# A decoder layer step on one core: a projection that multiplies tiles as they arrive, and an expert stage whose down product takes 4-byte operands

## The reference

```
h  = rms_norm(x, g_mix)                       # rows, then times g_mix by column
p  = h @ w_in                                 # 1024 x 3072: qd kd vd | qs ks vs, 512 columns each
o  = concat(diff_attention(qd, kd, vd), stick_breaking_attention(qs, ks, vs))
x1 = x + o @ w_out
h2 = rms_norm(x1, g_ffn)
gates: top 1 of 4 groups, then top 2 of its 4 experts, softmax weights
y  = x1 + sum over the 2 experts of gate * ((silu(h2 @ w_gate[e]) * (h2 @ w_up[e])) @ w_down[e])
out = rms_norm(y, g_final)                    # and k and v rows of both kinds are outputs
```

## Time and profile before

| what | us |
|---|---|
| three timed executions | 1706.43, 1712.57, 1714.13 (median 1712.57) |
| the profiled execution, its own time | 1703.53 |
| its span, first to last instruction | 1701.7 |
| PE busy, mean granted clock | 1345.3, 0.901 |
| DVE, ACT, POOL busy | 817.5, 721.3, 267.8 |
| first product of project to its last result | 38.95 to 371.27 |
| attention of both kinds, mix_out, route | 378 to 1258 |
| experts, from the first gate_up to the last store's issue | 1280.68 to 1631.35 |
| combine, to the end | 1636 to 1701.7 |
| DMA | 319.76 MB, 188 GB/s over the span |

### The profile page before, as it was taken

How to read it: one execution, slowest core, us unless ns; L and a number is a source line. 1 busy time by engine, 2 the same in 40 slices (tenths; PEclk the granted TensorE clock), 3 DMA queues, 4 the chain that set the end, 5 groups by cost and what they waited for, 6 DMA issues and landing times. The chain is left out here.

```text
span 1701.7 us, 28599 instructions
## 1 busy us (share of the span) xinstructions
PE 1345.3 (79%) x8942; PEld 1004.4 (59%) x8942; DVE 817.5 (48%) x1142; ACT 721.3 (42%) x1115; POOL 267.8 (16%) x200
## 2 busy tenths in 40 slices
PE   6999999977878887858887878599428888899920
PEld 4777787755545555435555554488326667677720
DVE  7022112104645445527574758444346665567735
ACT  6022212204545364535454545223106676677711
POOL 1000000000000000000000000000004545566544
PEclk6999999998999899979999999799758999999975
DMA  5333123217867776367777778354136797643257
GB/s 190 96 118 124 68 69 112 79 57 254 254 216 260 219 247 218 118 210 250 225 215 247 230 246 271 91 173 149 74 140 244 294 354 301 234 176 108 91 193 300
DMA packets 165910, 319.76 MB, mean 188 GB/s; under 512 B 21607, under 2 KB 59018, under 8 KB 161674
## 3 DMA queue, kind: packets, MB, share of 16 engines
q1 hardware_dynamic: 152922, 275.06, 48.5%
q0 software_dynamic: 7200, 26.22, 4.3%
q10 hardware_dynamic: 5648, 16.78, 2.5%
HBM read 312.82 MB, written 56.03 MB: 217 GB/s over the span
## 5 line engine op out<-in xcount | busy, mean ns | idle before, releaser
L2011 PE MATMUL gate_up_ps<-w_gate_up_split,slot_rows_T 128*128 128x512 f32 x768 | 194.5, 411 | 31.8 <-DVE slot_rows_T L2063 31.7
L2055 DVE TENSOR_TENSOR w_gate_up_split<-w_gate_up,w_gate_up_split 128x2048 fp32r<-128x2048 f32 x64 | 143.8, 2289 | 131.7 <-ACT w_gate_up_split L2109 131.7
L1979 POOL TENSOR_TENSOR w_down_split<-w_down,w_down_split 128x2048 fp32r<-128x2048 f32 x32 | 170.5, 5328 | 162.1 <-ACT w_down_split L2117 162.1
L933 PE MATMUL turns_and_scores_ps<-ident,pages 128*128 128x128 f32 (+1 forms) x1088 | 151.6, 284 | 55.8 <-DMA pages<-in_cache_s 27.2
L2011 PEld LDWEIGHTS gate_up_ps<-w_gate_up_split,slot_rows_T 128*128 128x128 f32 x768 | 149.3, 198 | 70.2 <-DVE slot_rows_T L2063 38.6
L933 PEld LDWEIGHTS turns_and_scores_ps<-ident,pages 128*128 128x128 f32 (+1 forms) x1088 | 124.0, 148 | 99.1 <-issue 98.8
L255 PE MATMUL proj_ps<-w_in_hi,h_T_hi 128*128 128x512 f32 x432 | 173.6, 402 | 9.4 <-DVE w_in_lo L305 9.4
L255 PE MATMUL proj_ps<-w_in_lo,h_T_hi 128*128 128x512 f32 x432 | 170.8, 395 | 0.0
L255 PE MATMUL proj_ps<-w_in_hi,h_T_lo 128*128 128x512 f32 x432 | 170.6, 395 | 0.0
L2109 ACT ACTIVATE w_gate_up_split<-w_gate_up 128x2048 fp32r x64 | 119.0, 1907 | 120.3 <-DMA w_gate_up<-in_w_up 92.8
L350 ACT ACTIVATE proj_rows<-proj_ps,sum_squares 128x512 f32<-128x512 f32 x54 | 37.0, 688 | 276.2 <-PE proj_ps L255 259.1
(11 more groups left out here) (227 smaller groups left out, 2138.4 us busy)
## 6 DMA issues: line engine op xcount, KB each, us to landing
pages<-in_cache_d SPq DMA_DIRECT2D x256, 256.0 KB, 3.1
pages<-in_cache_s SPq DMA_DIRECT2D x256, 256.0 KB, 3.1
w_gate_up<-in_w_gate SPq DMA_DIRECT2D x32, 1024.0 KB
w_gate_up<-in_w_up SPq DMA_DIRECT2D x32, 1024.0 KB
w_down<-in_w_down SPq DMA_DIRECT2D x32, 1024.0 KB
scratch_moe_out<-expert_out ACTq DMA_DIRECT2D x32, 512.0 KB
w_in_now<-in_w_in SPq DMA_DIRECT2D x48, 256.0 KB, 4.6
x_tiles<-in_x SPq DMA_DIRECT2D x9, 512.0 KB, 10.5
```

Of the source, the lines that this page charges most:

```text
L933: last = pe.transpose(kT_ps[:, KIND_BLOCKS * e + b, 0:n], rows[0:n, e, b, :], t.ident[0:n, 0:n])
L1979: pool.tensor_tensor(dn_split[:, u, 1, :, :], w_dn[:, bass.ds(at, 1), :, :].rearrange("p a k n -> p (a k) n"), dn_split[:, u, 0, :, :].bit ...
L2011: last = pe.matmul(gu_ps[:, u, :], xT[:, u, a, k, :], gu_split[:, u, b, k, :], start=(k == 0 and m == 0), stop=(k == KC - 1 and m == 2))
L2055: dve.tensor_tensor(gu_split[:, u, 1, at, :].rearrange("p k (c n) -> p k c n", c=2), raw[:, at, :, :], gu_split[:, u, 0, at, :].bitcast(F3 ...
```

## The change

In project:

- The order of groups is k, q, v for each kind. Nine x tiles go through three places. PE turns tiles 0 and 1, then multiplies tile 0 with the first group; in each later step of the first group it turns the tile two ahead.
- g_mix goes into w_in and no longer into h: ACT scales by g when it makes the high part, DVE when it makes the low part. x is split straight from PSUM by ACT and DVE.
- w_in_hi and w_in_lo have two copies, and the next group's pieces are split one per step, during the first eight steps of a group.
- q is made as columns: a slice of 128 columns of w_in is the stationary operand, the x columns of all tiles are the moving one, in chunks of 512, 512 and 128; 12 steps for a group of q, no transposes. A column's factor (root of its row times 1/8) is needed along the free axis: ACT makes nine diagonal blocks, PE multiplies ones by them (1152 columns, 4-byte operands), ACT keeps the result, DVE multiplies by it.
- The bias tables' products and copies stand in steps 3 to 7 after the first group, their spreading on SyncE behind the first q group. The loop is written out.

In experts: the down product takes the raw w_down and the activations as 4-byte operands, four products of 512 in place of twelve; there is no split of w_down and none of the activations. Raw weights have four places, with one place number; the load of down waits for the down product of tile t - 4. PE loads the place number itself. keep_act comes before keep_y on ACT. In route the place is the turn number and 3 (six instructions fewer).

```diff
+GROUPS = [(kind, role) for kind in range(2) for role in ROLE_NAMES]
+X_PLACES = 3
+PJ_BANKS = 3
...
+        w_hi = sb("w_in_hi", [P, 2, KC, BANK], F32R)
+        w_lo = sb("w_in_lo", [P, 2, KC, BANK], F32R)
...
+                load_x(0)
+                for k in range(KC):
+                    load_w(0, k)
+                    if k in (2, 5):
+                        load_x(k // 2)
...
+                def product(step):
+                    g, a, c = step
+                    n = number[step]
+                    if g == 0:
+                        pe.wait_ge(lo_done, 2 * a + 2)
...
+                        if step == of_group[g][0]:
+                            pe.wait_ge(w_lo_done, g * KC + k + 1)
+                        if GROUPS[g][1] == "q":
+                            c0, c1 = CHUNKS[c]
+                            at = slice(a * P, a * P + P)
+                            for m, (w, h) in enumerate(((w_hi, hT_hi), (w_hi, hT_lo), (w_lo, hT_hi))):
+                                last = pe.matmul(pj_ps[:, n % PJ_BANKS, 0:c1 - c0], w[:, g % 2, k, at], h[:, k, c0:c1],
+                                                 start=(k == 0 and m == 0), stop=(k == KC - 1 and m == 2))
+                        else:
+                            at = slice(a * P, a * P + P)
+                            for m, (h, w) in enumerate(((hT_hi, w_hi), (hT_lo, w_hi), (hT_hi, w_lo))):
+                                last = pe.matmul(pj_ps[:, n % PJ_BANKS, :], h[:, k, at], w[:, g % 2, k, :],
+                                                 start=(k == 0 and m == 0), stop=(k == KC - 1 and m == 2))
...
+                turn_x(0)
+                turn_x(1)
+                unturned = None
+                for step in steps:
+                    g, n, _ = step
+                    product(step)
+                    if g == 0 and n + 2 < TILES:
+                        turn_x(n + 2)
+                    if unturned:
+                        turn_k(unturned)
+                    unturned = step if step in turned else None
+                    if number[step] >= last_of(0):
+                        after = number[step] - last_of(0)
+                        if after < len(CHUNKS) and after < 2:
+                            rstd_across(after)
+                        elif after == 2:
+                            rstd_across(2)
+                        elif after < 3 + H_DIFF + 1:
+                            tables.bias(pe, after - 3, row_kept)
...
+                def low_w(g, k):
+                    dve.wait_ge(w_hi_done, g * KC + k + 1)
+                    dve.scalar_tensor_tensor(w_lo[:, g % 2, k, :], w_raw[:, k, :], g_T[:, k:k + 1],
+                                             w_hi[:, g % 2, k, :].bitcast(F32), ALU.mult, ALU.subtract)\
+                       .then_inc(w_lo_done, 1)
+
...
+                    dve.tensor_tensor(qkT[:, m % 3, 0:c1 - c0], pj_ps[:, n % PJ_BANKS, 0:c1 - c0], rstd_row[:, c0:c1],
+                                      ALU.mult).then_inc(cols_kept, 1)
...
+                act.wait_ge(g_loaded, 16)
+                high_x(0)
+                for k in range(4):
+                    high_w(0, k)
+                high_x(1)
+                for k in range(4, KC):
+                    high_w(0, k)
+                high_x(2)
...
+                    if g == 0 and n + 2 < TILES:
+                        high_x(2 * n + 4)
+                        high_x(2 * n + 5)
+                        square(n + 2)
+                    if g == 1 and at < len(CHUNKS):
+                        keep_across(at)
+                    if step in in_rows:
+                        keep_rows(step)
+                    if g == 0:
+                        diagonal(n)
+                    if at < KC and g + 1 < len(GROUPS):
+                        high_w(g + 1, at)
+                    if g == 1 and at == len(CHUNKS) + 1:
+                        tables.exps_of_sums(act)
...
+W_PLACES = 4
...
-                    dn_lo.reached(sp, tile - DN_PLACES)
+                    y_done.reached(sp, tile - W_PLACES, 1)
...
-                    u = tile % 2
+                    u, at = tile % 2, place(pe, tile)
                     aT_kept.reached(pe, tile)
-                    dn_lo.reached(pe, tile)
+                    pe.wait_ge(dn_loaded[tile % W_PLACES], 16 * (tile // W_PLACES) + 16)
                     for c in range(2):
                         y_kept[c].reached(pe, tile - 1)
+                        own_wait(pe, t)
                         for k in range(FK):
-                            for m, (a, b) in enumerate(PRODUCTS):
-                                last = pe.matmul(y_ps[:, c, :], aT[:, u, a, k, :],
-                                                 dn_split[:, u, b, k, c * BANK:(c + 1) * BANK],
-                                                 start=(k == 0 and m == 0), stop=(k == FK - 1 and m == 2))
+                            last = pe.matmul(y_ps[:, c, :], aT[:, u, k, :],
+                                             w_dn[:, bass.ds(at, 1), k, c * BANK:(c + 1) * BANK]
+                                             .rearrange("p a n -> p (a n)"), start=(k == 0), stop=(k == FK - 1))
                         last.then_inc(y_done.sem, 1)
...
-                    split_dn(tile)
                     swish(tile)
                     if tile + 1 < MOE_TILES:
                         split_rows(tile + 1)
+                    keep_act(tile)
                     if tile:
                         keep_y(tile - 1)
-                    keep_act(tile)
                     if tile:
```

More of the change, by code:

```diff
@@ L38 @@
 BANK = 512
-PROJ_G = 3 * MIX_W // BANK
 BLOCKS = MIX_W // P
@@ L110, in sem @@
             return sems[-1]
[L112 to L117, removed]
-        g_T = sb("g_mix_T", [P, KC])
[L119 to L123, removed]
+        steps = project_steps()
@@ new lines, in project @@
+        number = {step: n for n, step in enumerate(steps)}
+        in_rows = {step: n for n, step in enumerate(s for s in steps if GROUPS[s[0]][1] != "q")}
+        in_cols = {step: n for n, step in enumerate(s for s in steps if GROUPS[s[0]][1] == "q")}
+        of_group = [[s for s in steps if s[0] == g] for g in range(len(GROUPS))]
+        turned = {step: n for n, step in enumerate(s for s in steps if GROUPS[s[0]][1] == "k")}
+        staged = {step: n for n, step in enumerate(s for s in steps if GROUPS[s[0]][1] != "v")}
@@ L147, in project, with last_of @@
         w_view = t.w_in.rearrange("(k p) n -> k p n", p=P)
[L148 to L156, removed]
+        tables = Tables(nc, ctx, sems, t, [xT_ps[:, n, :] for n in range(2)])
+        def last_of(g):
+            return number[of_group[g][-1]] + 1
         with nc.Block() as block:
@@ L234, in _, with turn_k @@
                         last.then_inc(xT_done, 1)
[L235 to L241 removed]
+                def turn_k(step):
+                    r, n = in_rows[step], turned[step]
+                    pe.wait_ge(rows_kept, r + 1)
+                    if n >= 3:
+                        pe.wait_ge(tr_kept, n - 2)
@@ L298, in _ @@
[L298 to L313 removed]
+                    at, cols = slice(4 * half, 4 * half + 4), slice(n * P, n * P + P)
@@ new lines, in _ @@
+                low_x(0)
+                for k in range(4):
+                    low_w(0, k)
+                low_x(1)
+                for k in range(4, KC):
+                    low_w(0, k)
+                low_x(2)
+                low_x(3)
+                unturned = None
+                for step in steps:
+                    g, n, _ = step
+                    at = number[step] - number[of_group[g][0]]
+                    if g == 0 and n + 2 < TILES:
+                        low_x(2 * n + 4)
+                        low_x(2 * n + 5)
+                    if unturned:
+                        keep_turned(unturned)
+                    unturned = step if step in turned else None
+                    if step in in_cols:
+                        keep_columns(step)
+                    if at < KC and g + 1 < len(GROUPS):
+                        low_w(g + 1, at)
+                    if step == of_group[0][-1]:
+                        tables.widen(dve)
+                    after = number[step] - last_of(0) - 3
+                    if 0 <= after < H_DIFF + 1:
+                        tables.keep(dve, after)
+                    if g == 2 and at == 1:
+                        tables.rest(dve)
```

424 lines of the change are left out of this document (202 added, 222 removed).

## The result

| | before | changed |
|---|---|---|
| median of four executions, us | 1713.09 (1706.43 to 1714.13) | 1655.43 (1652.47 to 1659.02) |
| profiled execution, span | 1701.7 | 1650.6 |
| PE, DVE, ACT, POOL busy | 1345, 817, 721, 268 | 1339, 800, 662, 141 |

The ratio is 0.967, 95% interval 0.964 to 0.970: 57.7 us by the medians, 51.1 between the two profiled executions, where 23.6 were forecast and 1685 us predicted.

The account below looks back on a forecast made before the run. TensorE (PE) was taken to bound both changed stages. Projection -15.6 us (-26.6 - 13.4 - 2.4 + 5.1 + 21.7) and experts -8.0 gave -23.6, from a mean of 1709.2 to 1685.6, stated as 1685; range 1662 to 1710.

Parts of the forecast that it names:

- the price of the narrow product: Projection, q as columns: 192 products of 128 columns at 0.17 us each, between 0.118 and 0.227; 32.6 us, so +21.7.
- the tile's period: Expert stage: PE's own loop sets 10.57 us a tile, 317.1 for 30 tiles instead of 326.3, -9.2.
- the case by columns: Rival in the projection: narrow products cost by their columns, 192 x 0.113 us less, 1664 us in all; chance 0.08.
- the ring: Expert stage: turn_act, keep_act, keep_y, store, ACT's and DVE's splits, low rows, next gate_up; 10.3 us, just under PE's 10.37.
- The slower rival: Expert stage: PE's register load ahead of down empties PE's queue; at 1.2 us a tile 38 us, 1723; chance 0.07.
- a sign of being wrong: Expert stage: a ring on ACT and DVE that ends after PE was listed among what would show the prediction wrong.
- The start: Projection: first product at 12.3 us instead of 38.95, -26.6 us; bounds 10 and 17.
- Group edges: Projection: two copies of split w_in and later turning of k rows remove PE waits; -13.4 us, bounds 0 and -15.
- transposes: Projection: 18 fours fewer for q, 14 fours more for x, at 0.60 us a four; -2.4 us.
- rstd and bias: Projection: bias products now among the products, 3.2 us, and the rstd row in two passes, 1.9; together +5.1 us.
- SyncE's order: Projection: bias spreading holds SyncE some 17 us behind the first q group, v has about 27 us of slack; no cost.
- Four places: Expert stage: loads wait only for tile t-4 and nothing on POOL; all late weights and the clock drops after them go.

## Why the prediction was wrong

The direction was right, and so was what the projection gains by. Two steps failed, both the same way: the price of the narrow product, and the tile's period, where the bound itself was the wrong one. Had either come as forecast, the time would have been in the range. By the table, 23.6 + 11.3 (projection) + 9.1 (tiles) + 3.4 (first tile) - 0.4 (tail) = 47.0 us, and the 4.1 between the stages (variation, and up to 1.25 of it route) make 51.1.

*The narrow product: the first of the two failures.* "between the other two no row decides, and I take the middle, 0.17". It measured 0.112 us, so 192 cost 21.5 us and not 32.6: q as columns +10.6, not +21.7. Those are 11.1 us, next to the 11.3 by which the projection's end was off. The row nearest in kind decided after all: 4-byte passes of the same 128 columns with the same weight load stood at 0.118. I had put it as the low bound and mixed it with a case (0.227) for which only the equal weight load spoke. What came lies between the case by columns (0.057) and my middle: columns count down to a floor, and at 128 the floor decides. The chance of 0.08 for the cheaper side was far too small. The 81 ns that the Trainium skill gives for 128 columns ("TensorE: Matmul & The Clock Gate", Back-to-back issue gap) is below the measured 112, as its 131 is below 227, and still nearer than my middle.

*The tile's period: the second, and here the mechanism too.* "So 9.57 + 0.80 + 0.2 = 10.57 a tile". PE's list measures 10.01, and it does not set the period: the ring through ScalarE and VectorE does, at 10.27. The parts:
- 9.57 was 9.95 less the 0.38 of idle time that the row showed. But turn_act to gate_up was 0.76 between starts and is 0.14 where nothing waits: the wait was 0.62. Idle time in a row is counted from the modelled end of the instruction before, which for two short transposes is 0.24 later than the next could start. Right was 9.33 (5.58 + 0.79 + 2.82 + 0.14).
- +0.80 for down compared 8 x 0.44 with 12 x 0.227. By starts the old down took 2.82, the new 3.43: +0.61. The eight passes were taken 0.09 too dear (3.52), the twelve products 0.10 too cheap (2.72).
- +0.2 for the register load: turn_rows to down is 0.87 for 0.79, so 0.08 at most. Three more cost nothing in the late tiles and up to 0.5 in some new ones. So 9.33 + 0.61 + 0.08 = 10.02, and the list measures 10.01. The slower rival (1.2 us a tile) did not come.
- The ring, "10.3", has the right number, in part by luck. Its path was right: from turn_act to the gate_up after the next it has 0.38 + 10.26 = 10.64, and the trace 10.66. But I closed it over one tile, with turn_act 0.38 ahead of gate_up. It closes over two: (10.66 + 9.87) / 2 gives 10.26 and the trace 10.27. Over one tile, with the 0.14 by which turn_act stands ahead of the late gate_up, the same path gives 10.52, which is the longer tile of each pair. I let the ring hide under a PE list that was too long. It is the bound, which I had named as a sign of being wrong.

*The start.* 13.52 for 12.3: the table load, 1.28 us, was missing from my sum, but w_in's fourth piece ahead of x held the start as well. Taking away the first alone gave 0.18 us, the second after it 2.2. "The low clock in the first 5 us of products is paid in both kernels" did not hold either: the products stand 0.43 us apart from 38.95 to 43.81 before and only from 13.52 to 15.38 in the changed kernel, 1.3 us in its favour. *Group edges, transposes, rstd and bias.* By the sum they come out within about 1.4 us of the forecast: from the first product to the last result 330.8 us were measured, and 332.3 - 13.4 - 2.4 + 5.1 + 10.6 gives 332.2; the 1.3 of the low clock lie in that difference, so the items are not separated by it. PE never waits for w_in_lo after the first product. *SyncE's order* cost nothing, as said.

*Four places.* That late weights and dropped clocks would go was right; that the old lateness was POOL's alone is not borne out: with half of POOL's work the tiles took 318.3 and with none of it and three places 320.7, where 30 tiles at the old steady 9.95 are 298.5.

*Not foreseen:* gate_up of tile 1 comes 3.4 us sooner after the first load of weights, and route's six instructions fewer, which I had put at nothing.

## What to carry to other kernels

Take the period of an engine's list from starts of instructions where nothing waits, not from a period less the idle time that a row shows: here that alone was 0.24 us a tile. Where two loops share a stage, work out the ring that runs through the other engines over as many tiles as there are buffers, divide by that number, and compare it with PE's list: the longer one is the period, and here tiles that alternate were the ring's sign. Before a difference of a few us is put down to a change, look how much the same stage varies in runs that leave it alone: here 6.3 us in the old expert stage and 13 between the stages. Price an unknown shape by the row that has the same kind of weight load and the same number of columns, and do not average it with a case that no row supports.

## What the runs showed of the hardware

A product with a 128 x 128 weight load, at full clock, follows the one before after 0.112 us for 128 columns, 0.147 for 320, 0.173 for 384 and 0.227 for 512 (x_T and w_in in fp32r). One chunk of 512 and one of 128 (0.339) thus cost more than two of 320 (0.294). A product on 4-byte operands stands in the trace as two passes; one of 512 columns takes 0.43. A register load on PE has a median of 0.30 us and takes up to 0.99. Ahead of down one load cost at most 0.08 in each of the 30 tiles; four cost no more than one in 20 of them, and up to 0.5 more in ten. The first ACT_TABLE_LOAD takes 1.28 us and stands at ScalarE's first activation: with one on a constant it ran at 2.02, while the first data was still on its way.
